# Spatial gating in three blocks: the norm's offset enters the base through column sums, and ScalarE normalises the second half's rows

## The chip, the cores and the metric

The kernel runs on one core of a Trainium2 chip. The metric is the device time of one execution in microseconds (us); a time quoted below is the median of three runs unless it is the profiled execution's own. The engines are TensorE (PE, with its weight loads as PEld), VectorE (DVE), ScalarE (ACT), GpSimd (POOL) and SyncE (SP), which here only issues DMAs.

## What is computed

The program applies three blocks of a network to 1024 positions of 1024 features. The change touches only the third, and in it the spatial gating:

```
def layer_norm(x, g, b):
    mu = jnp.mean(x32, axis=-1, keepdims=True)
    var = jnp.mean(jnp.square(x32 - mu), axis=-1, keepdims=True)
    y = (x32 - mu) * lax.rsqrt(var + EPS)
    return (y * g.astype(jnp.float32) + b.astype(jnp.float32)).astype(x.dtype)

def spatial_gating(u, v, ln_g, ln_b, w_s, b_s):
    """gMLP SGU: u * (W_s LN(v) + b) with W_s mixing positions inside each 128-chunk, per channel group."""
    v = layer_norm(v, ln_g, ln_b)
    vc = v.reshape(B, S // CHUNK, CHUNK, G_A, C // G_A)
    s = jnp.einsum('gpq,bcqge->bcpge', w_s, vc) + b_s.T[:, :, None]
    return u * s.reshape(B, S, C)
```

`v` is 1024 positions by 2048 channels, in 8 chunks of 128 positions and 16 groups of 128 channels. For an element, W_s LN(v) is the sum over positions q of w[p,q] (n[q] g + b), with n the normalised row. The part with `b` is b times the sum of w[p,q] over q, and does not depend on the chunk.

## The kernel before, in words

`spatial_gating` (line 3885) is called twice, for half 0 and half 1 of the channels (8 groups, 1024 channels each), with a dense layer between and one behind. Each call is a stage with a block of its own: every engine has its list of instructions, and the next stage starts when all have ended theirs. A tile t is one chunk of 128 positions; there are 8 tiles, and most buffers are doubled (`v_`, `raw`, `y`, the PSUM banks 2p and 2p+1), the gates `uz` tripled.

Per tile, the engines do this:

- **SyncE** (from line 3897) loads `raw` (the rows of v; all 2048 channels in half 0, since the variance needs them, 1024 in half 1) and `uz`, the factor u silu(z). `load_rows(t)` waits until norm(t-2) is through; `load_gates(t)` waits for gate(t-3). In its list come rows 0, the bias, `g`, `b`, the spatial weights `ws`, gates 0, rows 1, gates 1 and 2, and then for t from 2: rows t, gates t+1. Rows t+1 therefore stand behind gates t+1.
- **ScalarE** lays `base` into the two PSUM banks of the tile (`lay_base`, line 3941), in half 0 takes the sum of squares of `raw` and its root (`squares`, line 3948), and rounds the result to `high` (`rounds`, line 3956). In the loop the order is lay_base(t+1), squares(t+2), rounds(t).
- **VectorE** normalises (`norm`, line 3995) and multiplies the mixed result by `uz` (`gate`, line 4009), in the order norm(t+1), gate(t). `norm` is two three-input instructions of 128x1024: (raw + less) times g at line 3998, then times rstd plus b at line 4006. In half 0 the reciprocal of the root stands between them (line 4003). `less` is minus the mean; `rstd` is left over from half 0 for half 1.
- **TensorE** mixes: eight plain float32 matmuls of 128x128 per tile (line 4049), which add into the base.
- **POOL** subtracts `high` from the result to give `low` (line 3981, 128x1024); gate(t+2) waits for it.

At the start TensorE spreads the bias over 128 partitions by matmuls with one contracted row (line 4038), from the bias split in two parts, and ScalarE copies the result to `base` (line 3964).

```
                    v.wait_ge(sig(f"loaded{p}"), j * 16 + 16)
                    v.wait_ge(sig("mixed"), t * 2 + 2)
```

These two waits head `norm`: `mixed` is preset to 4, so that norm(0) and norm(1) do not wait for a matmul.

Of the kernel before, what the change touches and what calls it, by code (L numbers as in the profile page):

```python
# [8 lines left out]
P = 128  # L9
# [3 lines left out]
NT = SEQ // P  # L13
HALF = 512
# [6 lines left out]
ALU = mybir.AluOpType  # L21
ACT = mybir.ActivationFunctionType
# [655 lines left out]
class Stage:  # L678
# [15 lines left out]
    def sb(self, name, shape, dt=F32):  # L694
        return self.ctx.enter_context(self.core.nc.sbuf_tensor(f"{self.name}_{name}_sb", shape, dt))
# [3190 lines left out]
def spatial_gating(core, half, sums, less, rstd, high, low, weights):  # L3886

    nc, d = core.nc, core.d
    with Stage(core, f"sgu{half}") as st:
# [1 line left out]
        ws = sb("ws", [P, GH, P])  # L3891
        bias = [st.sb(f"bias{i}", [1, GH * P], F32R) for i in range(2)]
        one = st.sb("one", [1, P], F32R)
        g, b_ = (sb(n, [P, DH])[:, :] for n in ("g", "b"))
        v_ = [sb(f"v{p}", [P, DH]) for p in range(2)]
        raw = [sb(f"raw{p}", [P, DA if half == 0 else DH]) for p in range(2)]
        uz = [sb(f"uz{i}", [P, GH, P]) for i in range(3)]
# [2 lines left out]
        var = sb("var", [P, NT]) if half == 0 else None  # L3900
        mine = slice(half * DH, (half + 1) * DH)
        gs = slice(half * GH, (half + 1) * GH)
        base = sb("base", [P, GH * P])
        with nc.Block() as block:
            @block.sync
            def _(sp):
                def load_rows(t, p, j):
                    if t >= 2:
                        sp.wait_ge(sig("normed"), t - 1)
                    of = d["rows3"][ds(t * P, P), VA:VA + DA] if half == 0 else d["rows3"][ds(t * P, P), VA + DH:VA + DA]  # L3910
                    sp.dma_start(raw[p][:, :], of).then_inc(sig(f"loaded{p}"), 16)

                def load_gates(t):
                    if t >= 3:
                        sp.wait_ge(sig("done"), t)
                    sp.dma_start(uz[t % 3][:, :, :], d["uz"][mine, ds(t * P, P)].rearrange("(k p) t -> p k t", p=P)
                                 ).then_inc(sig(f"gates{t % 3}"), 16)
                load_rows(0, 0, 0)
                sp.dma_start(bs, d["b_spatial"][0:1, gs, :].rearrange("o g t -> o (g t)")).then_inc(sig("bias_in"), 16)
                for to, of in ((g, d["sgu_g"][:, mine]), (b_, d["sgu_b"][:, mine])):  # L3920
                    sp.dma_start(to, of).then_inc(sig("affine_in"), 16)
                sp.dma_start(ws[:, :, :], d["w_spatial"][:, gs, :]).then_inc(sig("spatial_in"), 16)
                load_gates(0)
                load_rows(1, 1, 0)
                load_gates(1)
                load_gates(2)
                for t in range(2, NT):
                    load_rows(t, t % 2, t // 2)
                    if t + 1 < NT:
                        load_gates(t + 1)  # L3930

            @block.scalar
            def _(a):
# [6 lines left out]
                def lay_base(t, p):  # L3940
# [4 lines left out]
                        ins = nc.scalar.activation(core.acc[2 * p + q][:, :], base[:, q * HALF:(q + 1) * HALF], ACT.Copy)  # L3945
                    ins.then_inc(sig("based"), 1)

                def squares(t, p, j):
                    a.wait_ge(sig(f"loaded{p}"), j * 16 + 16)
                    nc.scalar.activation(core.acc_quad, raw[p][:, :], ACT.Square, bias=less[:, ds(t, 1)],  # L3950
# [8 lines left out]

                if half == 0:  # L3960
                    squares(0, 0, 0)
                a.wait_ge(sig("spread"), 1)
                for q in range(2):
                    ins = nc.scalar.activation(base[:, q * HALF:(q + 1) * HALF], core.acc[q][:, :], ACT.Copy)
# [2 lines left out]
                lay_base(0, 0)  # L3967
                if half == 0:
                    squares(1, 1, 0)
                for t in range(NT):  # L3970
                    if t + 1 < NT:
                        lay_base(t + 1, (t + 1) % 2)
                    if half == 0 and t + 2 < NT:
                        squares(t + 2, t % 2, t // 2 + 1)
                    rounds(t, t % 2)

            @block.gpsimd
# [8 lines left out]
            def _(v):  # L3986
                v.sem_inc(sig("done"), 2)
                v.sem_inc(sig("split"), 2)
                if half == 0:
# [2 lines left out]
                    nc.vector.tensor_scalar(less[:, :], less[:, :], -1.0 / DA, None, ALU.mult).then_inc(sig("less"), 1)  # L3992
                    v.wait_ge(sig("less"), 2)

                def norm(t, p, j):
                    v.wait_ge(sig(f"loaded{p}"), j * 16 + 16)
                    v.wait_ge(sig("mixed"), t * 2 + 2)
                    nc.vector.scalar_tensor_tensor(out=v_[p][:, :], in0=raw[p][:, mine] if half == 0 else raw[p][:, :],
                                                   scalar=less[:, ds(t, 1)], in1=g, op0=ALU.add,
                                                   op1=ALU.mult).then_inc(sig("centred"), 1)  # L4000
                    if half == 0:
                        v.wait_ge(sig("rooted"), t + 1)
                        nc.vector.reciprocal(rstd[:, ds(t, 1)], rstd[:, ds(t, 1)]).then_inc(sig("inverted"), 1)
                        v.wait_ge(sig("inverted"), t + 1)
                    v.wait_ge(sig("centred"), t + 1)
                    nc.vector.scalar_tensor_tensor(out=v_[p][:, :], in0=v_[p][:, :], scalar=rstd[:, ds(t, 1)], in1=b_,
                                                   op0=ALU.mult, op1=ALU.add).then_inc(sig("normed"), 1)

                def gate(t, p):
                    v.wait_ge(sig("split"), t + 1)  # L4010
# [21 lines left out]
            @block.tensor  # L4032
            def _(pe):
                pe.sem_inc(sig("mixed"), 4)
                pe.wait_ge(sig("bias_low"), 1)
                for q in range(2):
                    for i in range(2):
                        mm = nc.tensor.matmul(core.acc[q], one[:, :], bias[i][:, q * HALF:(q + 1) * HALF], start=i == 0, stop=i == 1)
                mm.then_inc(sig("spread"), 1)
                pe.wait_ge(sig("spatial_in"), 16)  # L4040

                def body(t, p, j):
                    pe.wait_ge(sig("based"), t + 1)
# [314 lines left out]
```

## Time and profile before

| | us |
|---|---|
| median of 3 runs | 4650.26 (4645.92 to 4656.61) |
| profiled execution, its own time | 4649.78 |
| its span, first to last instruction | 4648.0 |
| TensorE busy | 4284.1 (92%) |
| VectorE busy | 1886.4 (41%) |
| ScalarE busy | 1343.2 (29%) |
| POOL busy | 1154.4 (25%) |
| stretch 4094 to 4157.7, TensorE / VectorE / ScalarE / POOL busy | 28.9 / 35.3 / 38.6 / 21.0 |
| stretch 4282.5 to 4342.3, the same | 30.4 / 43.5 / 19.1 / 19.8 |

The two stretches are the two calls of `spatial_gating`. Times are microseconds from the start of the span. A row of the order of time reads: start, duration, engine, line, operation, names written and read, shapes, count, and in brackets how long the engine had been idle before it and what ended that. Where a row stands for several instructions, the duration runs from the first start to the last end. A mean granted TensorE clock of 1.00 is 2.4 GHz, 0.50 is 1.2 GHz.

### The profile page before, as it was taken

How to read it: one execution, taken by the hardware profiler on the slowest of the kernel's cores; microseconds unless marked ns; L12 is line 12 of the kernel's file. 1: busy time of each engine (PE TensorE's matmuls, PEld its weight loads, DVE VectorE, ACT ScalarE, POOL GpSimd, SP SyncE). 2: the span in 40 equal slices, each digit the busy share in tenths (PEclk: the TensorE clock that was granted, in tenths of full speed). 3: DMA queues.
4: the chain of work that ended last, by engine and by line, in shares of the span. 5: the costliest groups of instructions: out<-in, count | busy, mean ns of one | idle time of the engine just before them, and what ended most of it. 6: DMA issues, size and time to landing. Idle time of an engine off the chain costs nothing. (4 is left out here: it accounts for less than half of the span.)

```text
span 4648.0 us, 53906 instructions
## 1 busy us (share of the span) xinstructions
PE 4284.1 (92%) x21558; PEld 3501.7 (75%) x21558; DVE 1886.4 (41%) x3289; ACT 1343.2 (29%) x2357; POOL 1154.4 (25%) x575
## 2 busy tenths in 40 slices
PE   8999999879995888699999999999999999967897
PEld 6888777656775887468888877888788888856776
DVE  3022666652595665435424424000133333346433
ACT  3121333432313443421001012112244444343112
POOL 2220100331152666222222212212111111122313
PEclk9999999879997999899999999999999999978899
DMA  3243111331523110311111112333333333266422
GB/s 123 102 157 102 34 27 26 118 97 50 208 87 99 42 31 17 110 46 46 55 46 46 55 37 89 113 138 104 90 84 104 104 107 95 67 218 191 154 82 91
DMA packets 276997, 417.23 MB, mean 90 GB/s; under 512 B 50439, under 2 KB 184120, under 8 KB 270862
## 3 DMA queue, kind: packets, MB, share of 16 engines
q1 hardware_dynamic: 221022, 313.20, 21.8%
q10 hardware_dynamic: 53104, 94.92, 5.5%
q0 software_dynamic: 2624, 5.68, 0.5%
q8 instruction: 172, 2.82, 0.3%
q14 instruction: 75, 0.61, 0.0%
HBM read 290.31 MB, written 123.40 MB: 89 GB/s over the span
## 5 line engine op out<-in xcount | busy, mean ns | idle before, releaser
L163 POOL TENSOR_TENSOR weights_wlow<-weights_raw,weights_whigh 128x1024 fp32r<-128x1024 f32 (+1 forms) x236 | 695.6, 2969 | 2450.3 <-ACT weights_whigh L154 2450.3
L154 ACT ACTIVATE weights_whigh<-weights_raw 128x1024 fp32r<-128x1024 f32 (+1 forms) x236 | 266.6, 1164 | 1170.8 <-PE acc L313 787.8
L313 PE MATMUL acc<-h_high_half,weights_whigh 128*128 128x512 f32 x1408 | 556.8, 395 | 20.9 <-POOL weights_wlow L163 17.1
L313 PE MATMUL acc<-h_low_half,weights_whigh 128*128 128x512 f32 x1408 | 553.7, 393 | 0.0
L313 PE MATMUL acc<-h_high_half,weights_wlow 128*128 128x512 f32 x1408 | 553.5, 393 | 0.0
L313 PEld LDWEIGHTS acc<-h_high_half,weights_whigh 128*128 128x128 f32 x1408 | 266.0, 189 | 89.2 <-POOL weights_wlow L163 18.4
L3575 PE MATMUL acc<-h_high_half,weights_whigh 128*128 128x512 f32 x768 | 331.3, 431 | 0.0
L313 PEld LDWEIGHTS acc<-h_high_half,weights_wlow 128*128 128x128 f32 x1408 | 265.9, 189 | 59.3 <-issue 1.0
L313 PEld LDWEIGHTS acc<-h_low_half,weights_whigh 128*128 128x128 f32 x1408 | 265.6, 189 | 59.3
L3575 PE MATMUL acc<-h_low_half,weights_whigh 128*128 128x512 f32 x768 | 302.2, 393 | 0.0
L3575 PE MATMUL acc<-h_high_half,weights_wlow 128*128 128x512 f32 x768 | 300.8, 392 | 0.0
L316 PE MATMUL acc<-weights_whigh,h_low_half 128*128 128x512 f32 x768 | 300.3, 391 | 0.0
L316 PE MATMUL acc<-weights_wlow,h_high_half 128*128 128x512 f32 x768 | 300.3, 391 | 0.0
L316 PE MATMUL acc<-weights_whigh,h_high_half 128*128 128x512 f32 x768 | 300.3, 391 | 0.0
L313 PE MATMUL acc<-y_high_half,weights_whigh 128*128 128x512 f32 x448 | 181.8, 406 | 28.2 <-DVE x_here L4138 17.7
L2023 DVE TENSOR_TENSOR x_here<-x_here,acc 128x512 f32<-128x512 f32 x80 | 55.0, 687 | 371.2 <-PE acc L313 371.2
L313 PE MATMUL acc<-hidden_high,weights_whigh 128*128 128x512 f32 x512 | 199.2, 389 | 0.0
L313 PE MATMUL acc<-hidden_high,weights_wlow 128*128 128x512 f32 x512 | 199.2, 389 | 0.0
L3483 DVE SCALAR_TENSOR_TENSOR gated_biased_sb<-gated_near_ends_sb,gated_slope_sb,acc 128x384 f32<-128x384 f32 x40 | 24.6, 614 | 412.3 <-DMA gated_end_sb<-rows 271.0
L313 PE MATMUL acc<-y_high_half,weights_wlow 128*128 128x512 f32 x448 | 178.8, 399 | 0.0
L313 PE MATMUL acc<-y_low_half,weights_whigh 128*128 128x512 f32 x448 | 178.6, 399 | 0.0
L3500 ACT ACTIVATE gated_probs_sb<-gated_biased_sb,gated_result_sb 128x192 f32<-128x192 f32 (+2 forms) x192 | 85.4, 446 | 290.4 <-DVE gated_result_sb L3490 290.1
(555 smaller groups left out, 8238.9 us busy)
## 6 DMA issues: line engine op xcount, KB each, us to landing
weights_raw<-w_cols SPq DMA_DIRECT2D x94, 512.0 KB, 4.8
weights_raw<-w_ff SPq DMA_DIRECT2D x64, 512.0 KB, 3.7
weights_raw<-w_rows SPq DMA_DIRECT2D x30, 1024.0 KB, 7.2
att<-gated_result_sb SPq DMA_DIRECT2D x96, 130.0 KB, 2.2
merge_o_sb<-att SPq DMA_DIRECT2D x24, 520.0 KB, 6.6
rows<-norm_square ACTq DMA_DIRECT2D x48, 256.0 KB, 2.1
weights_raw<-w_out SPq DMA_DIRECT2D x24, 512.0 KB, 3.8
cols<-first_out ACTq DMA_DIRECT2D x40, 256.0 KB, 2.0
```

What stands on the lines that cost most here:

```text
L154: self.core.nc.scalar.activation(high[p][:, half * (KC // 2):(half + 1) * (KC // 2), :], raw[half], ACT.Copy).then_inc(self.core.sem("roun ...
L163: self.core.nc.gpsimd.tensor_tensor(low[p][:, hs, :], raw[half], high[p][:, hs, :].bitcast(F32), ALU.subtract).then_inc(self.core.sem("wei ...
L313: mm = nc.tensor.matmul(core.acc[b][:, :], wt[p][:, k, c * P:(c + 1) * P], h[:, k, half * HALF:(half + 1) * HALF], start=first, stop=final)
L316: mm = nc.tensor.matmul(core.acc[b][:, 0:width], h[:, k, b * P:(b + 1) * P], wt[p][:, k, :], start=first, stop=final)
L2023: return core.nc.vector.tensor_tensor(to, to, acc, ALU.add)
L3483: nc.vector.scalar_tensor_tensor(out=biased, in0=mask, scalar=self.slope[p][:, st["dilation"]:st["dilation"] + 1], in1=acc, op0=ALU.mult, ...
L3500: nc.scalar.activation(self.probs[g % 2][:, u, 0:w], self.biased[g % 2][:, u, 0:w], ACT.Exp, bias=result[:, u, AE + 1:AE + 2], scale=AE ** ...
L3575: mm = nc.tensor.matmul(core.acc[b][:, :], wt[n % 2][:, k, c * P:(c + 1) * P], of[:, k, half * HALF:(half + 1) * HALF], start=(k == 0 and ...
```

## The change

`b` is loaded as one row instead of 128. TensorE first multiplies a column of ones with the spatial weights (two matmuls of 512 columns, one output row), which gives the column sums; ScalarE copies them to the buffer `columns`; TensorE adds `b` times these sums to the spread bias, group by group (eight matmuls with one contracted row), before ScalarE takes the base. `norm` then needs no offset: in half 0 it is the reciprocal, a tensor_scalar (plus less, times rstd) and a multiplication by `g`, all behind the root; in half 1 ScalarE computes raw times rstd plus `shift` (`shift` is less times rstd) in place in `raw`, in the new function `centre`, and VectorE multiplies by `g`. The wait for the matmul of two tiles before stays with VectorE.

```diff
--- before.py
+++ after.py
@@ -3891,7 +3891,7 @@
         ws = sb("ws", [P, GH, P])
         bias = [st.sb(f"bias{i}", [1, GH * P], F32R) for i in range(2)]
         one = st.sb("one", [1, P], F32R)
-        g, b_ = (sb(n, [P, DH])[:, :] for n in ("g", "b"))
+        g, b_ = sb("g", [P, DH])[:, :], sb("b", [1, DH])[:, :]
         v_ = [sb(f"v{p}", [P, DH]) for p in range(2)]
         raw = [sb(f"raw{p}", [P, DA if half == 0 else DH]) for p in range(2)]
         uz = [sb(f"uz{i}", [P, GH, P]) for i in range(3)]
@@ -3900,7 +3900,8 @@
         var = sb("var", [P, NT]) if half == 0 else None
         mine = slice(half * DH, (half + 1) * DH)
         gs = slice(half * GH, (half + 1) * GH)
-        base = sb("base", [P, GH * P])
+        base, columns = sb("base", [P, GH * P]), y[1][0:1, :]
+        shift = sb("shift", [P, NT]) if half else None
         with nc.Block() as block:
             @block.sync
             def _(sp):
@@ -3917,7 +3918,7 @@
                                  ).then_inc(sig(f"gates{t % 3}"), 16)
                 load_rows(0, 0, 0)
                 sp.dma_start(bs, d["b_spatial"][0:1, gs, :].rearrange("o g t -> o (g t)")).then_inc(sig("bias_in"), 16)
-                for to, of in ((g, d["sgu_g"][:, mine]), (b_, d["sgu_b"][:, mine])):
+                for to, of in ((g, d["sgu_g"][:, mine]), (b_, d["sgu_b"][0:1, mine])):
                     sp.dma_start(to, of).then_inc(sig("affine_in"), 16)
                 sp.dma_start(ws[:, :, :], d["w_spatial"][:, gs, :]).then_inc(sig("spatial_in"), 16)
                 load_gates(0)
@@ -3945,6 +3946,12 @@
                         ins = nc.scalar.activation(core.acc[2 * p + q][:, :], base[:, q * HALF:(q + 1) * HALF], ACT.Copy)
                     ins.then_inc(sig("based"), 1)
 
+                def centre(t, p, j):
+                    a.wait_ge(sig(f"loaded{p}"), j * 16 + 16)
+                    a.wait_ge(sig("less"), 1)
+                    nc.scalar.activation(raw[p][:, :], raw[p][:, :], ACT.Identity, scale=rstd[:, ds(t, 1)],
+                                         bias=shift[:, ds(t, 1)]).then_inc(sig("centred"), 1)
+
                 def squares(t, p, j):
                     a.wait_ge(sig(f"loaded{p}"), j * 16 + 16)
                     nc.scalar.activation(core.acc_quad, raw[p][:, :], ACT.Square, bias=less[:, ds(t, 1)],
@@ -3959,6 +3966,12 @@
 
                 if half == 0:
                     squares(0, 0, 0)
+                else:
+                    centre(0, 0, 0)
+                a.wait_ge(sig("column_sums"), 1)
+                for q in range(2):
+                    ins = nc.scalar.activation(columns[:, q * HALF:(q + 1) * HALF], core.acc[2 + q][0:1, :], ACT.Copy)
+                ins.then_inc(sig("columns"), 1)
                 a.wait_ge(sig("spread"), 1)
                 for q in range(2):
                     ins = nc.scalar.activation(base[:, q * HALF:(q + 1) * HALF], core.acc[q][:, :], ACT.Copy)
@@ -3967,11 +3980,15 @@
                 lay_base(0, 0)
                 if half == 0:
                     squares(1, 1, 0)
+                else:
+                    centre(1, 1, 0)
                 for t in range(NT):
                     if t + 1 < NT:
                         lay_base(t + 1, (t + 1) % 2)
                     if half == 0 and t + 2 < NT:
                         squares(t + 2, t % 2, t // 2 + 1)
+                    if half and t + 2 < NT:
+                        centre(t + 2, t % 2, t // 2 + 1)
                     rounds(t, t % 2)
 
             @block.gpsimd
@@ -3992,19 +4009,20 @@
                     nc.vector.tensor_scalar(less[:, :], less[:, :], -1.0 / DA, None, ALU.mult).then_inc(sig("less"), 1)
                     v.wait_ge(sig("less"), 2)
 
+                if half:
+                    nc.vector.tensor_tensor(shift[:, :], less[:, :], rstd[:, :], ALU.mult).then_inc(sig("less"), 1)
+
                 def norm(t, p, j):
-                    v.wait_ge(sig(f"loaded{p}"), j * 16 + 16)
                     v.wait_ge(sig("mixed"), t * 2 + 2)
-                    nc.vector.scalar_tensor_tensor(out=v_[p][:, :], in0=raw[p][:, mine] if half == 0 else raw[p][:, :],
-                                                   scalar=less[:, ds(t, 1)], in1=g, op0=ALU.add,
-                                                   op1=ALU.mult).then_inc(sig("centred"), 1)
                     if half == 0:
+                        v.wait_ge(sig(f"loaded{p}"), j * 16 + 16)
                         v.wait_ge(sig("rooted"), t + 1)
                         nc.vector.reciprocal(rstd[:, ds(t, 1)], rstd[:, ds(t, 1)]).then_inc(sig("inverted"), 1)
                         v.wait_ge(sig("inverted"), t + 1)
+                        nc.vector.tensor_scalar(v_[p][:, :], raw[p][:, mine], less[:, ds(t, 1)], rstd[:, ds(t, 1)], ALU.add,
+                                                ALU.mult).then_inc(sig("centred"), 1)
                     v.wait_ge(sig("centred"), t + 1)
-                    nc.vector.scalar_tensor_tensor(out=v_[p][:, :], in0=v_[p][:, :], scalar=rstd[:, ds(t, 1)], in1=b_,
-                                                   op0=ALU.mult, op1=ALU.add).then_inc(sig("normed"), 1)
+                    nc.vector.tensor_tensor(v_[p][:, :], v_[p][:, :] if half == 0 else raw[p][:, :], g, ALU.mult).then_inc(sig("normed"), 1)
 
                 def gate(t, p):
                     v.wait_ge(sig("split"), t + 1)
@@ -4032,12 +4050,22 @@
             @block.tensor
             def _(pe):
                 pe.sem_inc(sig("mixed"), 4)
+                pe.wait_ge(sig("spatial_in"), 16)
+                for q in range(2):
+                    mm = nc.tensor.matmul(core.acc[2 + q][0:1, :], core.ones[:, 0:1], ws[:, 4 * q:4 * q + 4, :].rearrange("p g t -> p (g t)"),
+                                          start=True, stop=True)
+                mm.then_inc(sig("column_sums"), 1)
                 pe.wait_ge(sig("bias_low"), 1)
                 for q in range(2):
                     for i in range(2):
-                        mm = nc.tensor.matmul(core.acc[q], one[:, :], bias[i][:, q * HALF:(q + 1) * HALF], start=i == 0, stop=i == 1)
+                        nc.tensor.matmul(core.acc[q], one[:, :], bias[i][:, q * HALF:(q + 1) * HALF], start=i == 0, stop=i == 1)
+                pe.wait_ge(sig("affine_in"), 32)
+                pe.wait_ge(sig("columns"), 1)
+                for gg in range(GH):
+                    cs = slice(gg * P, (gg + 1) * P)
+                    mm = nc.tensor.matmul(core.acc[gg // 4][:, gg % 4 * P:(gg % 4 + 1) * P], b_[0:1, cs], columns[:, cs],
+                                          start=False, stop=True, skip_group_check=True)
                 mm.then_inc(sig("spread"), 1)
-                pe.wait_ge(sig("spatial_in"), 16)
 
                 def body(t, p, j):
                     pe.wait_ge(sig("based"), t + 1)
```

Three places show how the instructions stand. On **TensorE** at the start of each of the two stages (`sgu_ws` are the spatial weights, `sgu_one` ones, `sgu_y` holds the column sums):

```order
-L4038 MATMUL acc<-sgu_bias_sb,sgu_one_sb 128x512 x4
-L4049 MATMUL acc<-sgu_ws_sb,sgu_v_sb 128x128 x64
-L3904 UNCONDITIONAL_BRANCH
+L4050 UNCONDITIONAL_BRANCH
+L4055 MATMUL acc<-sgu_ws_sb,ones_here 1x512 x2
+L4061 MATMUL acc<-sgu_bias_sb,sgu_one_sb 128x512 x4
+L4066 MATMUL acc<-sgu_y_sb,sgu_b_sb 128x128 x8
+L4077 MATMUL acc<-sgu_ws_sb,sgu_v_sb 128x128 x64
```

Two matmuls now stand ahead of the bias and eight behind it; the 64 mixing matmuls are as before.

On **VectorE** in half 0, norm(2), gate(1) and norm(3), before:

```order
L3998 SCALAR_TENSOR_TENSOR sgu_v_sb<-sgu_raw_sb,va_less,sgu_g_sb 128x1024
L4003 RECIPROCAL va_rstd<-va_rstd 128x1
L4006 SCALAR_TENSOR_TENSOR sgu_v_sb<-sgu_v_sb,va_rstd,sgu_b_sb 128x1024
L4015 TENSOR_TENSOR sgu_y_sb<-acc,sgu_uz_sb 128x512 x2
L3998 SCALAR_TENSOR_TENSOR sgu_v_sb<-sgu_raw_sb,va_less,sgu_g_sb 128x1024
```

and in the change:

```order
L4020 RECIPROCAL va_rstd<-va_rstd 128x1
L4022 TENSOR_SCALAR sgu_v_sb<-sgu_raw_sb,va_less,va_rstd 128x1024
L4025 TENSOR_TENSOR sgu_v_sb<-sgu_v_sb,sgu_g_sb 128x1024
L4033 TENSOR_TENSOR sgu_y_sb<-acc,sgu_uz_sb 128x512 x2
L4020 RECIPROCAL va_rstd<-va_rstd 128x1
```

The first long instruction has moved behind the reciprocal, and so behind the root on ScalarE.

On **ScalarE** in half 1, from the start of the stage, in the change:

```order
L3937 ACTIVATE sgu_bias_sb<-sgu_y_sb 1x1024
L3952 ACTIVATE sgu_raw_sb<-sgu_raw_sb,sgu_shift_sb,va_rstd 128x1024
L3973 ACTIVATE sgu_y_sb<-acc 1x512 x2
L3977 ACTIVATE sgu_base_sb<-acc 128x512 x2
L3946 ACTIVATE acc<-sgu_base_sb 128x512 x2
L3952 ACTIVATE sgu_raw_sb<-sgu_raw_sb,sgu_shift_sb,va_rstd 128x1024
L3946 ACTIVATE acc<-sgu_base_sb 128x512 x2
L3952 ACTIVATE sgu_raw_sb<-sgu_raw_sb,sgu_shift_sb,va_rstd 128x1024
L3965 ACTIVATE y_high_half<-sgu_y_sb 128x8x128
```

The instructions of line 3952 and the pair of line 3973 are new; before, the rounding of a tile (there line 3958) stood directly behind the laying of the next.

## Rows read from the trace of the kernel before

**Rows 1.** The page: its first line.

```profile
span 4648.0 us, 53906 instructions
```

**Rows 2.** Order of time, first half, POOL: start us, us, engine line op, names, shapes.

```profile
4124.67 2.72 POOL L3981 TENSOR_TENSOR y_low_half<-sgu_y_sb,y_high_half 128x1024 fp32r<-128x1024 f32 x1 [1.97 <-ACT y_high_half L3958]
...
4155.21 2.34 POOL L3981 TENSOR_TENSOR y_low_half<-sgu_y_sb,y_high_half 128x1024 fp32r<-128x1024 f32 x1 [1.45 <-ACT y_high_half L3958]
```

**Rows 3.** Order of time, second half, POOL.

```profile
4307.24 2.34 POOL L3981 TENSOR_TENSOR y_low_half<-sgu_y_sb,y_high_half 128x1024 fp32r<-128x1024 f32 x1 [3.45 <-ACT y_high_half L3958]
...
4339.72 2.34 POOL L3981 TENSOR_TENSOR y_low_half<-sgu_y_sb,y_high_half 128x1024 fp32r<-128x1024 f32 x1 [1.08 <-ACT y_high_half L3958]
```

**Rows 4.** Order of time, first matmul behind the second half, TensorE.

```profile
4342.56 0.77 PE L313 MATMUL acc<-y_high_half,weights_whigh 128*128 128x512 f32 x1 [4.73 <-PEq L3904]
```

**Rows 5.** Order of time, first half, VectorE: gate(0), tile 3, gates 2 and 6.

```profile
4113.43 1.28 DVE L4015 TENSOR_TENSOR sgu_y_sb<-acc,sgu_uz_sb 128x512 f32<-128x512 f32 x2
...
4123.89 1.28 DVE L4006 SCALAR_TENSOR_TENSOR sgu_v_sb<-sgu_v_sb,va_rstd,sgu_b_sb 128x1024 f32<-128x1024 f32 x1
4125.10 1.28 DVE L4015 TENSOR_TENSOR sgu_y_sb<-acc,sgu_uz_sb 128x512 f32<-128x512 f32 x2
...
4148.96 1.28 DVE L4015 TENSOR_TENSOR sgu_y_sb<-acc,sgu_uz_sb 128x512 f32<-128x512 f32 x2
```

**Rows 6.** Order of time, first half, ScalarE, around the root of tile 3.

```profile
4121.22 1.97 ACT L3950 ACTIVATE acc<-sgu_raw_sb,va_less 128x2048 f32<-128x2048 f32 x1 [0.29 <-DMA sgu_raw_sb<-rows]
...
4123.35 0.30 ACT L3953 ACTIVATE va_rstd<-sgu_var_sb,eps_here 128x1 f32<-128x1 f32 x1
4123.55 1.04 ACT L3958 ACTIVATE y_high_half<-sgu_y_sb 128x1024 fp32r<-128x1024 f32 x1
```

**Rows 7.** Order of time, second half, VectorE.

```profile
4298.04 1.28 DVE L4015 TENSOR_TENSOR sgu_y_sb<-acc,sgu_uz_sb 128x512 f32<-128x512 f32 x2
...
4307.29 3.37 DVE L4006 SCALAR_TENSOR_TENSOR sgu_v_sb<-sgu_v_sb,va_rstd,sgu_b_sb 128x1024 f32<-128x1024 f32 x1
...
4333.85 1.27 DVE L4015 TENSOR_TENSOR sgu_y_sb<-acc,sgu_uz_sb 128x512 f32<-128x512 f32 x2
```

**Rows 8.** Instructions on the tile sgu_ws: issue of its loads, and landing.

```profile
L3922 SPq DMA_DIRECT2D sgu_ws_sb<-w_spatial x2: 432/497/562, 4097.1 to 4284.4; - x2
...
DMA to landing us min/median/max: 8.0/8.0/8.1
```

**Rows 9.** Order of time, first norm instruction of each half, VectorE.

```profile
4103.89 1.28 DVE L3998 SCALAR_TENSOR_TENSOR sgu_v_sb<-sgu_raw_sb,va_less,sgu_g_sb 128x1024 f32<-128x1024 f32 x1 [1.41 <-DMA sgu_b_sb<-sgu_b]
...
4291.09 1.28 DVE L3998 SCALAR_TENSOR_TENSOR sgu_v_sb<-sgu_raw_sb,va_less,sgu_g_sb 128x1024 f32<-128x1024 f32 x1 [2.77 <-DMA sgu_b_sb<-sgu_b]
```

**Rows 10.** Order of time, float32 matmuls of 512 columns elsewhere, TensorE.

```profile
1947.82 6.69 PE L3180 MATMUL acc<-second_sums_sb,ones_here 128*128 128x512 f32 x8 [29.25 <-DVE second_sums_sb L3247]
```

**Rows 11.** Windows: start:end, us, busy PE, PEld, DVE, ACT, POOL, granted clock, DMA, GB/s.

```profile
4346.00:4347.00 1.00, 1.00 (x4) 0.76 (x4) 0.00 (x0) 0.00 (x0) 0.00 (x0) 0.69 0.88 295
...
1953.00:1954.00 1.00, 1.00 (x4) 0.42 (x2) 0.74 (x2) 0.19 (x1) 0.00 (x0) 0.56 1.00 401
```

**Rows 12.** Order of time, first half, ScalarE: the copy of the base.

```profile
4104.66 1.06 ACT L3964 ACTIVATE sgu_base_sb<-acc 128x512 f32<-128x512 f32 x2
```

**Rows 13.** Order of time, first half, TensorE.

```profile
4102.53 2.07 PE L4038 MATMUL acc<-sgu_bias_sb,sgu_one_sb 1*128 1x512 f32 x4 [10.10 <-DVE sgu_bias_sb L4020]
4106.98 3.76 PE L4049 MATMUL acc<-sgu_ws_sb,sgu_v_sb 128*128 128x128 f32 x16 [2.38 <-ACT acc L3945]
...
4125.65 2.05 PE L4049 MATMUL acc<-sgu_ws_sb,sgu_v_sb 128*128 128x128 f32 x16 [0.89 <-ACT acc L3945]
```

**Rows 14.** Instructions of lines 1456 and 3263, VectorE (ns min/median/max, first and last start).

```profile
L1456 DVE TENSOR_SCALAR norm_square<-short_in,short_taps x6: 752/754/4031, 265.2 to 376.5; 128x1024 f32<-128x1024 f32 x6
...
L3263 DVE TENSOR_TENSOR second_y_sb<-second_y_sb,second_rstd_sb x4: 1215/1216/1216, 1963.4 to 1969.1; 128x1024 f32<-128x1024 f32 x4
```

**Rows 15.** DMA issues in the second half: engine op xcount, KB, us to landing.

```profile
sgu_raw_sb<-rows SPq DMA_DIRECT2D x8, 512.0 KB, 4.8
```

## The prediction

> **What bounds the kernel now.** I read the page first, for the span [rows 1], then the order of time of each engine over the two stretches in which the function `spatial_gating` runs, 4094 to 4158 us (first half of the channels) and 4282 to 4342 us (second half). Both are stages of their own: the last instruction of each is the last subtraction on GpSimd (POOL), ending at 4157.55 in the first [rows 2] and at 4342.06 in the second [rows 3], and TensorE's first matmul of the next stage starts 0.5 us later [rows 4]. So a microsecond won or lost in either stage is one of the whole time, and nothing else in the program changes.
>
> The **first half** is a loop over loads. The row load of tile t+1 stands on SyncE behind the gate load of that tile, which waits for the gate of tile t-2. So gate(0) lets rows 3 be loaded, these feed norm(3), which VectorE runs ahead of gate(2); gate(2) releases rows 5, and so on. From the rows: gate(0) ends at 4114.71 [rows 5], the squares of tile 3 start at 4121.22, when the DMA landed [rows 6], 6.51 later. Squares and root take 2.43, to 4123.65 [rows 6]; the second norm instruction starts 0.24 behind the root (4123.89) and the gate 1.21 behind that; the gate is 1.28 [rows 5]. 6.51 + 2.43 + 0.24 + 1.21 + 1.28 = 11.67 per two tiles, as gate(0) to gate(2) in the trace.
>
> The **second half** is bound by VectorE and POOL together. The second norm instruction takes 3.37 us where it starts 0.05 behind POOL's subtraction [rows 3, 7], against 1.28 alone [rows 5]; POOL's ends at 4309.59, VectorE's at 4310.66. An instruction with two SBUF inputs thus waits until POOL has finished, while gates, which read PSUM, stay at 1.28. Six gates lie 4333.85 - 4298.04 = 35.81 us apart, some 5.97 per tile, of which 2.1 is this wait.
>
> **Part 1: the start of each stage.** Before, TensorE needed only the bias to build the base. Now it first needs `ws`, the spatial weights, then column sums, ScalarE's copy, eight outer products and only then the base. `ws` was issued fifth and took 8.0 us to land, about 4105.2 and 4292.4 [rows 8]. The load of `b` ahead of it shrinks from 512 KB to 4 KB, so I let `ws` land when `b` did: about 4103.8 and 4291.0 [rows 9]. Bounds: no gain at all, 1.4 later in each half; I take the nearer row, since the order of issue stays.
>
> From there: two plain float32 matmuls of 512 columns. Four such take 6.69 with the clock mostly at 0.50 [rows 10, 11], so two take 3.4 and some 0.4 until the last result. Copying the sums is a pair of ScalarE copies as in [rows 12], 1.1 with its start. The four bias matmuls, 2.07 before [rows 13], lie beside that copy (3.4 + 1.7 = 5.1, against 5.0 for the copy). Then eight 128x128 float32 matmuls: 3.76 at the lower clock, 2.05 at the full one [rows 13]. TensorE comes cold (1.2 GHz). In [rows 11] the clock rose about 4 us after unbroken work began (start 4342.56 in [rows 4]), and after 6.1 us in the other case (start 1947.82). So the eight cost between 2.05 and 3.75; with a rise in their first third I take 2.4. TensorE is done 7.5 after the landing (7.1 to 8.9). Then the base copy and the laying of tile 0, a pair of copies each [rows 12], with their starts 2.3. Base laid at 4103.8 + 9.8 = 4113.6 and 4291.0 + 9.8 = 4300.8.
>
> *First half.* Squares(1) stand on ScalarE behind that laying. 4113.6 + squares and root 2.43 + reciprocal 0.24 + scale 0.85 + multiplication 1.14 + gate 1.28 = 4119.5 for the end of gate(0), against 4114.71: **+4.8**. *Second half.* Norms 0 and 1 are ready or early, the mixing takes 3.76 cold, and the last half of the gate 0.7: 4300.8 + 0.1 + 3.75 + 0.7 = 4305.3, against 4298.04 + 1.28 = 4299.3: **+6.0**.
>
> **Part 2: the norm of the first half.** Removed: the subtraction with gain, which ran beside the squares and was hidden, and the second three-input instruction (1.28). Added behind the root: a tensor_scalar with two scalars and a multiplication of two tensors. The first is bounded by 0.75, what 128x1024 takes with one scalar, and by 1.28, a three-input instruction; the second scalar adds what it adds between the two-tensor and the three-input form, 1.216 against 1.28 [rows 5, 14], so 0.81, plus 0.04 to the next start. The multiplication is 1.22 [rows 14]. Alone this makes a loop 0.85 - 0.06 = 0.8 longer.
>
> But it moves the multiplication into POOL's way. After the root ScalarE rounds the previous tile, and POOL starts 1.02 after the root's end (4123.65 to 4124.67) [rows 2, 6]. Before, VectorE's instruction had started at +0.24, ahead of POOL. Now the scale ends and the multiplication starts at 0.24 + 0.85 = +1.09, which is 0.07 behind POOL; 0.05 was enough to make it wait in [rows 3, 7]. POOL runs 2.35 and VectorE ends 1.02 after it (4310.66 - 4309.59 = 1.07, less 0.06): 1.02 + 2.35 + 1.02 = +4.39, instead of +1.52. The loop grows by 2.87 to 14.54. Three loops lie between gate(0) and gate(6): 43.6 against 4148.96 - 4113.43 = 35.5 [rows 5], **+8.1**. The tail behind gate(6) stays.
>
> The Trainium skill, "VectorE: DVE Perf Modes", Rules for kernel authors, advises to minimise the number of instructions, as each is followed by a drain. By that alone half one gets eight instructions more and half two eight fewer, and this loop would grow by 0.8 only, which is the sum of the first rival. "GPSIMD Engine Reference", Key points, has VectorE share SBUF interfaces with POOL when it has two SBUF inputs or runs in a two-port mode; the two-input case is what the rows of the second half show, the other no row of these stages does.
>
> **Part 3: the norm of the second half.** ScalarE centres and scales in place (128x1024, as its rounding: 1.04 [rows 6]), VectorE multiplies once. ScalarE has room, two copies and a rounding being all that it did per tile. POOL again starts 1.0 behind the centring, but the multiplication starts 0.05 behind it and is through first; the wait of 2.1 goes and POOL waits 0.2 instead. What is late next is the load: 0.44 for SyncE, 4.8 to land [rows 15], centring 1.05, 0.05, multiplication 1.14, gate 1.28 = 8.76 per two tiles. Three loops 26.3 against 35.8: **-9.5**. The last mixing (3.76) is now less covered, **+0.5**. Shift (8x128 elements), less bytes, and memory: nothing, they lie in the idle start.
>
> **Sum:** 4.8 + 8.1 = +12.9 in the first half, 6.0 - 9.5 + 0.5 = -3.0 in the second, +9.9. The profiled execution took 4649.78, the median is 4650.26, 0.5 apart. I set the sum on the median: **4660 us**. About 0.2% (9.3 us) is what a measurement of this kernel can tell from no change, so the likeliest case lies almost on that line.
>
> **The rivals.**
> *A. The multiplication is ahead of POOL* (not slower). Place: the first half, 1.02 us behind each root. It decides at 70 ns: if the scale takes 0.74 or less, the multiplication takes the port first and POOL waits. For it: the margin is as small as that. Against: in half two a lead of 0.05 was enough for POOL. Loop 12.46, three 37.4, +1.9 in place of +8.1: total +3.7, 4654.
> *B. The clock goes up in the start and stays up.* The mixing is then 2.05: in the second half the first and the last are on the path, 3.4 less: +6.5, 4657. For it: long unbroken work in the start. Against: the later mixings of both halves lie between 2.05 and 3.8 [rows 13].
> *C. The start stays at the lower clock throughout*: 8.9 instead of 7.5, twice: +12.7, 4663. If `ws` gains nothing from the shorter queue either, 2.8 more, 4666.
> *D. The narrow matmuls are cheap*, a column sum costing like a bias matmul (0.5): each start 3.5 shorter, +2.9, 4653. Nothing in the rows speaks for it but the small outputs.
>
> **How the numbers follow.** The forecast has 0.55, A 0.2, B 0.08, C 0.07, D 0.05, and 0.05 remain for what I do not see, a gain included. The range reaches from just below D and A less a run's scatter (the three runs spread over 10.7 us) to C with the late weights and a little scatter: 4649 to 4668; the forecast's own is 4655 to 4665. Slower by over 0.2%: a little over half of the forecast, all of C, 0.39 or 0.40. Faster by over 0.2%: 0.06, from scatter and the unseen. Within 0.2%: 0.54.
>
> **What would show it.** In the new trace: (1) `ws` lands near 4103.8 and 4291.0, column sums take 3.4; (2) gate(0) ends at 4119.5 and, shifted by the first half, 6.0 later than before in the second; (3) the new multiplication of the first half takes 3.3 us from tile 3 on, gates 14.5 apart in pairs; if it takes 1.22 and POOL 2.7, A holds; (4) in the second half multiplications take 1.22 and gates come in pairs 8.8 apart. The prediction is wrong if the first half is less than 8 us longer or the second is longer than before.

## The result, and the profile after

The change takes 4662.57 us, median of 13 runs (4656.91 to 4670.89), the kernel before 4648.17 in 13 runs beside it. The ratio is 1.0028, interval 1.0020 to 1.0035, which is 9 to 16 us with 13.0 in the middle (the two medians lie 14.4 apart): slower, and the interval begins just at the 0.2% that the prediction takes as its line. Forecast were +9.9 and 4660.

The page of the profiled execution (its own time 4659.25): its first lines, busy time and share of the span.

```profile
span 4657.3 us, 53999 instructions
...
PE 4285.3 (92%) x21598; PEld 3499.3 (75%) x21598; DVE 1864.4 (40%) x3282; ACT 1352.4 (29%) x2369; POOL 1155.6 (25%) x575
...
DVE  3022666652595664434424424000133333346333
ACT  3121333432214443420010022122244444443212
POOL 2220100341153666112222222212111111122313
```

Less work for VectorE (1864 against 1886 us), little more for the others, and a span 9.3 us longer: the loss is waiting. The table splits it by hand from the orders of time below and from [rows 2, 3, 5, 7], each time counted from the first DMA issue of its stage (before 4095.26 and 4282.84, after 4090.76 and 4294.09).

| us | first half: before, after, forecast of the difference | second half: before, after, forecast |
|---|---|---|
| to the end of gate(0) | 19.5, 23.5 (+4.0), +4.8 | 16.5, 24.0 (+7.5), +6.0 |
| from there to the end of gate(6) | 35.5, 45.0 (+9.5), +8.1 | 35.8, 27.0 (-8.8), -9.5 |
| from there to POOL's last end | 7.3, 6.6 (-0.7), 0 | 6.9, 6.7 (-0.3), +0.5 |
| stage | 62.3, 75.1 (+12.8), +12.9 | 59.2, 57.7 (-1.6), -3.0 |

The two stages are 11.2 us longer together. Outside them this execution was 2 us shorter than the one before, in stretches that the change does not touch. A stage alone varies by one or two microseconds between executions of the same code: the second one of the change lasted 57.7 us here and 58.2 to 59.8 in four runs below that leave it as it is. The -1.6 of the second half lies within that, the +12.8 of the first does not.

**The start.** TensorE in order of time, first half, then second:

```profile
4099.16 3.57 PE L4055 MATMUL acc<-sgu_ws_sb,ones_here 128*1 128x512 f32 x4 [11.23 <-DMA sgu_ws_sb<-w_spatial]
4102.66 1.41 PE L4061 MATMUL acc<-sgu_bias_sb,sgu_one_sb 1*128 1x512 f32 x4
4103.98 2.02 PE L4066 MATMUL acc<-sgu_y_sb,sgu_b_sb 1*128 1x128 f32 x16
4108.32 3.78 PE L4077 MATMUL acc<-sgu_ws_sb,sgu_v_sb 128*128 128x128 f32 x16 [2.33 <-ACT acc L3946]
...
4302.23 3.57 PE L4055 MATMUL acc<-sgu_ws_sb,ones_here 128*1 128x512 f32 x4 [9.16 <-DMA sgu_ws_sb<-w_spatial]
4305.73 2.07 PE L4061 MATMUL acc<-sgu_bias_sb,sgu_one_sb 1*128 1x512 f32 x4
4307.61 3.61 PE L4066 MATMUL acc<-sgu_y_sb,sgu_b_sb 1*128 1x128 f32 x16
```

and the clock over them (start:end, us, busy PE, granted clock, DMA share, GB/s):

```profile
4103.00:4104.00 1.00, 1.00 (x5) 0.92 1.15 315
4104.00:4106.00 2.00, 2.00 (x17) 1.00 1.21 309
...
4302.00:4305.00 3.00, 2.77 (x4) 0.50 1.07 355
4305.00:4308.00 3.00, 3.00 (x7) 0.50 1.17 308
4308.00:4311.20 3.20, 3.20 (x16) 0.50 0.30 114
```

The column sums start at 4099.16 and 4302.23, 8.4 and 8.1 us into the stage, when `ws` has landed (before, it landed 9.9 and 9.6 into the stage). The two of them cost 3.5 us together, at the lower clock throughout; four took 6.69 in [rows 10], where the clock rose towards the end. In the first half the mean of 0.92 from 4103 to 4104 puts the rise to 2.4 GHz at about 4103.15, 4.0 us after TensorE began, and the eight outer products took 2.02; TensorE was through after 6.8. In the second half the instructions are the same, but the clock stayed at 0.50 for the nine microseconds up to 4311.2 of unbroken work; the same eight took 3.61 and the block 9.0. The forecast had one value, 7.5, for both. The difference is no chance of one execution: in the five first halves with column sums the eight took 1.99 to 2.02, in the five second halves 3.61 or 3.62.

**The loop of the first half.** VectorE from gate(0) to gate(3), and gate(6); ScalarE around tile 3; POOL:

```profile
4112.93 1.28 DVE L4033 TENSOR_TENSOR sgu_y_sb<-acc,sgu_uz_sb 128x512 f32<-128x512 f32 x2
...
4123.57 0.16 DVE L4020 RECIPROCAL va_rstd<-va_rstd 128x1 f32<-128x1 f32 x1 [5.92 <-ACT va_rstd L3960]
4123.77 0.81 DVE L4022 TENSOR_SCALAR sgu_v_sb<-sgu_raw_sb,va_less,va_rstd 128x1024 f32<-128x1024 f32 x1
4124.61 3.27 DVE L4025 TENSOR_TENSOR sgu_v_sb<-sgu_v_sb,sgu_g_sb 128x1024 f32<-128x1024 f32 x1
4127.81 1.27 DVE L4033 TENSOR_TENSOR sgu_y_sb<-acc,sgu_uz_sb 128x512 f32<-128x512 f32 x2
...
4129.19 0.81 DVE L4022 TENSOR_SCALAR sgu_v_sb<-sgu_raw_sb,va_less,va_rstd 128x1024 f32<-128x1024 f32 x1
4130.04 1.23 DVE L4025 TENSOR_TENSOR sgu_v_sb<-sgu_v_sb,sgu_g_sb 128x1024 f32<-128x1024 f32 x1
...
4157.95 1.27 DVE L4033 TENSOR_TENSOR sgu_y_sb<-acc,sgu_uz_sb 128x512 f32<-128x512 f32 x2
```

```profile
4107.15 1.12 ACT L3946 ACTIVATE acc<-sgu_base_sb 128x512 f32<-128x512 f32 x2
...
4121.02 1.97 ACT L3957 ACTIVATE acc<-sgu_raw_sb,va_less 128x2048 f32<-128x2048 f32 x1 [4.70 <-DMA sgu_raw_sb<-rows]
...
4123.14 0.29 ACT L3960 ACTIVATE va_rstd<-sgu_var_sb,eps_here 128x1 f32<-128x1 f32 x1
4123.35 1.04 ACT L3965 ACTIVATE y_high_half<-sgu_y_sb 128x1024 fp32r<-128x1024 f32 x1
...
4136.37 1.97 ACT L3957 ACTIVATE acc<-sgu_raw_sb,va_less 128x2048 f32<-128x2048 f32 x1 [5.19 <-DMA sgu_raw_sb<-rows]
```

```profile
4124.46 2.34 POOL L3998 TENSOR_TENSOR y_low_half<-sgu_y_sb,y_high_half 128x1024 fp32r<-128x1024 f32 x1 [5.85 <-ACT y_high_half L3965]
4130.25 3.23 POOL L3998 TENSOR_TENSOR y_low_half<-sgu_y_sb,y_high_half 128x1024 fp32r<-128x1024 f32 x1 [3.45 <-ACT y_high_half L3965]
...
4163.52 2.34 POOL L3998 TENSOR_TENSOR y_low_half<-sgu_y_sb,y_high_half 128x1024 fp32r<-128x1024 f32 x1 [0.78 <-ACT y_high_half L3965]
```

The root of tile 3 ends at 4123.43; the reciprocal starts 0.14 behind it. The scale takes 0.81 and ends at 4124.58, the multiplication starts at 4124.61, 0.15 behind POOL (4124.46), and takes 3.27 instead of 1.23. In tile 4 (4130.04) it starts 0.21 ahead of POOL and takes 1.23, and POOL 3.23 instead of 2.34. Compare [rows 5, 2], where the instruction in this place had started 0.78 ahead of POOL.

**The loop of the second half.** VectorE at gate(0), tile 3 and gate(6); ScalarE and POOL at the same place:

```profile
4317.36 0.69 DVE L4033 TENSOR_TENSOR sgu_y_sb<-acc,sgu_uz_sb 128x512 f32<-128x512 f32 x1 [0.77 <-PE acc L4077]
...
4324.75 1.22 DVE L4025 TENSOR_TENSOR sgu_v_sb<-sgu_raw_sb,sgu_g_sb 128x1024 f32<-128x1024 f32 x1 [4.36 <-ACT sgu_raw_sb L3952]
4325.89 1.28 DVE L4033 TENSOR_TENSOR sgu_y_sb<-acc,sgu_uz_sb 128x512 f32<-128x512 f32 x2
...
4343.79 1.28 DVE L4033 TENSOR_TENSOR sgu_y_sb<-acc,sgu_uz_sb 128x512 f32<-128x512 f32 x2
```

```profile
4323.40 1.24 ACT L3952 ACTIVATE sgu_raw_sb<-sgu_raw_sb,sgu_shift_sb,va_rstd 128x1024 f32<-128x1024 f32 x1 [3.25 <-DMA sgu_raw_sb<-rows]
4324.55 1.04 ACT L3965 ACTIVATE y_high_half<-sgu_y_sb 128x1024 fp32r<-128x1024 f32 x1
```

```profile
4325.67 2.52 POOL L3998 TENSOR_TENSOR y_low_half<-sgu_y_sb,y_high_half 128x1024 fp32r<-128x1024 f32 x1 [4.09 <-ACT y_high_half L3965]
...
4349.41 2.34 POOL L3998 TENSOR_TENSOR y_low_half<-sgu_y_sb,y_high_half 128x1024 fp32r<-128x1024 f32 x1 [0.81 <-ACT y_high_half L3965]
```

The multiplication (4324.75, 1.22) has a lead of 0.92 on POOL, and POOL waits 0.2 in its place (2.52 instead of 2.34). The 3.37 of [rows 7] is gone. Centring takes 1.24, not the 1.04 of a rounding, and what it waited for was the load of the rows.

### The profile page after: what moved, and what is told of

The parts are those of the page before. It is cut to its first block and busy times, and to the rows that moved or that the text cites. A ratio compares the mean times of both kernels' runs of the same rounds, so it can differ in the third digit from the quotient of the medians.

```text
span 4657.3 us, 53999 instructions
## 1 busy us (share of the span) xinstructions
PE 4285.3 (92%) x21598; PEld 3499.3 (75%) x21598; DVE 1864.4 (40%) x3282; ACT 1352.4 (29%) x2369; POOL 1155.6 (25%) x575
```

## The experiments

All were timed in five rounds beside the kernel before, and the ratios are to that kernel; a difference in us is the ratio times its time. "Stage" is again from the first DMA issue to POOL's last end, in one profiled execution each.

**One half at a time.** With `new` choosing between the old and the new code of `norm`, of the start and of `centre` (in part; in the second of the two runs `new` is `half in (1,)`):

```diff
+        new = half in (0,)
...
+                    if not new:
+                        return norm_old(t, p, j)
```

> Only the first half of the channels is changed, the second is the kernel before. My theory (a longer start, and VectorE's multiplication held up by POOL's subtraction behind each root): the first stage lasts 75 us from its first DMA issue to POOL's last subtraction, as with the whole change, against 62.3 before, the second 59.2 as before; time 12.8 us above the kernel before. Rival (the halves disturb each other, or the loss lies elsewhere in the program): the time is as with the whole change or the two halves alone don't add up to it.

Measured: 1.0023 (1.0014 to 1.0032), +10.7 us; stages 75.6 and 58.6.

> Only the second half of the channels is changed. My theory: its longer start (+7.5 us to the first gate) is a little more than paid back by the wait for POOL that goes (-9): stage 57.7 us against 59.2, the time 1.5 us below the kernel before, which can't be told from no change. Rival (the start is all that counts, the loop being bound by loads before as well): 5 us or more above.

Measured: 0.9999 (0.9990 to 1.0009); second stage 58.2. (The first one, not changed, was 64.4 in this execution, 2 us longer than in the two others that have it unchanged.) So the whole loss belongs to the first half, and the second is worth nothing that can be told, its start eating what its loop gives: its stage lasted 57.7, 58.2, 59.1, 59.1 and 59.8 in the five executions with the code of the change, and 59.2 and 58.6 in two with the code before.

**POOL a little later.** One useless ScalarE copy ahead of each rounding of the first half (in part):

```diff
                 def rounds(t, p):
                     a.wait_ge(sig("done"), t + 3)
+                    if half == 0:
+                        nc.scalar.activation(idle[:, ds(t * 48, 48)], core.ones[:, 0:48], ACT.Copy)
```

> The whole change plus one small, useless ScalarE copy of 128x48 ahead of each rounding in the first half, some 0.25 us, so that POOL's subtraction starts that much later. My theory (the multiplication starts 0.15 us behind POOL and waits for it): the multiplication now starts first and takes 1.23 instead of 3.27 us, POOL waits, three loops get some 2 us shorter each, the first stage falls from 75 to about 69.5 us and the time to 6 us below the whole change, although work was added. Rival (the loop is longer because of the number and length of the instructions behind the root): the multiplication stays at 3.27, or the stage gets no shorter, and longer by up to 1 us.

Measured: 1.0021 (1.0012 to 1.0029), stage 76.1. By the letter this went to the rival. But the copy had moved POOL by only 0.13 us. The multiplication of tile 3:

```profile
4121.18 3.40 DVE L4028 TENSOR_TENSOR sgu_v_sb<-sgu_v_sb,sgu_g_sb 128x1024 f32<-128x1024 f32 x1
```

and POOL:

```profile
4121.16 2.35 POOL L4001 TENSOR_TENSOR y_low_half<-sgu_y_sb,y_high_half 128x1024 fp32r<-128x1024 f32 x1 [5.90 <-ACT y_high_half L3968]
```

POOL was still ahead, by 0.02 us, and VectorE waited for it to the end. The run had not separated the two theories, only brought the margin down to the edge. The next has three copies of 16 columns each.

> As the run with one small ScalarE copy ahead of the rounding in the first half, but with three copies of 128x16. One copy moved POOL's start only 0.13 us, to 0.02 ahead of the multiplication, which still waited (3.40 us). Three should move it some 0.4, to 0.25 us behind the multiplication's start. My theory (whichever of the two starts first holds the other up until it has ended): the multiplication takes 1.23 us and POOL's subtraction 3.2, the first stage falls from 75 to about 70 us, the time to 5 us below the whole change. Rival (POOL goes first whatever the order of start, or the length of the chain behind the root is what counts): the multiplication stays above 3 us, the stage at 75 or more.

Measured: 1.0017 (1.0008 to 1.0026), +7.9 us; first stage 69.4. VectorE and POOL at tile 3:

```profile
4124.63 0.81 DVE L4026 TENSOR_SCALAR sgu_v_sb<-sgu_raw_sb,va_less,va_rstd 128x1024 f32<-128x1024 f32 x1
4125.48 1.23 DVE L4029 TENSOR_TENSOR sgu_v_sb<-sgu_v_sb,sgu_g_sb 128x1024 f32<-128x1024 f32 x1
```

```profile
4125.64 3.28 POOL L4002 TENSOR_TENSOR y_low_half<-sgu_y_sb,y_high_half 128x1024 fp32r<-128x1024 f32 x1 [6.05 <-ACT y_high_half L3969]
```

Now the multiplication is 0.16 ahead; it takes 1.23, in all eight tiles, and POOL 3.28. With 0.4 us of work added per tile the stage is 5.7 us shorter than with the change (75.1), 6.7 shorter than with one copy. The place in the order of start, not the length of the chain, costs these microseconds. The intervals of the whole times of this run and the change overlap, so the stage carries the verdict; the three executions in which POOL goes first had 75.1, 75.6 and 76.1, so that the 5.7 stands clear of what a stage varies by. From gate(0) to gate(6) it is 38.9 us, between the 35.5 before and the 45.0 of the change: some 3.3 us of the loss are left with the order put right, and no run here splits them between the longer chain behind the root and the loads.

**Only the scaling behind the root** (in part; the first of the two stands ahead of the wait for the root).

```diff
+                        nc.vector.scalar_tensor_tensor(out=v_[p][:, :], in0=raw[p][:, mine], scalar=less[:, ds(t, 1)], in1=g,
+                                                       op0=ALU.add, op1=ALU.mult).then_inc(sig("centred"), 1)
...
+                        nc.vector.tensor_scalar(v_[p][:, :], v_[p][:, :], rstd[:, ds(t, 1)], None, ALU.mult).then_inc(sig("normed"), 1)
```

> The whole change, but in the first half VectorE computes (raw + less) g in one instruction beside the squares, as before the change, and behind the root only the multiplication by rstd (tensor_scalar with one scalar). My theory: that one takes 0.75 us, starts 0.24 behind the root and is through before POOL starts at 1.0; the loop is 11.67 - 0.53 = 11.1 us per two tiles, three loops 33.5 (before 35.5, with the change 45.0), the first stage 62.3 + 4.0 - 2.0 = 64.3 us, the whole time 1 us above the kernel before. Rival (column sums and what they delay are the main loss): the stage stays above 70 us.

Measured: 0.9999 (0.9990 to 1.0008); stages 62.2 and 59.8. VectorE at gate(0), the scaling of tile 3 and gate(6), and POOL's start in tile 3:

```profile
4113.10 1.33 DVE L4036 TENSOR_TENSOR sgu_y_sb<-acc,sgu_uz_sb 128x512 f32<-128x512 f32 x2
...
4123.77 0.76 DVE L4025 TENSOR_SCALAR sgu_v_sb<-sgu_v_sb,va_rstd 128x1024 f32<-128x1024 f32 x1
...
4146.81 1.28 DVE L4036 TENSOR_TENSOR sgu_y_sb<-acc,sgu_uz_sb 128x512 f32<-128x512 f32 x2
```

```profile
4124.56 2.37 POOL L3998 TENSOR_TENSOR y_low_half<-sgu_y_sb,y_high_half 128x1024 fp32r<-128x1024 f32 x1 [5.63 <-ACT y_high_half L3965]
```

The scaling takes 0.76 here (0.75 in the other tiles) and is through at 4124.53, 0.03 us before POOL comes; whether an instruction with one tensor from SBUF would have had to wait, this run does not show. From gate(0) to gate(6) it is 33.7 us, as expected (33.5); gate(0) ends 22.0 into the stage instead of 23.5, because the chain behind the root is shorter there too, which the expectation had left out. This removes the whole loss without touching the column sums.

**The offset without column sums.** One matmul per group, `b` on all partitions times the spatial weights, gives b times the sum directly (in part; `b` is loaded on 128 partitions again, and the bias matmuls wait for nothing else):

```diff
-                    mm = nc.tensor.matmul(core.acc[gg // 4][:, gg % 4 * P:(gg % 4 + 1) * P], b_[0:1, cs], columns[:, cs],
+                    mm = nc.tensor.matmul(core.acc[gg // 4][:, gg % 4 * P:(gg % 4 + 1) * P], b_[:, cs], ws[:, gg, :],
```

> The whole change, but the offset enters the base by one matmul per group straight from b on all 128 partitions (128x128 by 128x128, out[c,p] = sum over q of b[c] w[q,p]), without column sums, ScalarE's copy of them and outer products; the bias matmuls need not wait for the spatial weights; b is loaded as 512 KB again. My theory of the start (each step behind the landing of the weights delays the first gate): base laid 16.0 us behind the stage's start instead of 17.5 in the first half, 15.7 instead of 19.4 in the second, time 5 us below the whole change. Rival (the start is hidden by loads and the loops): no change against it.

Measured: 1.0009 (1.0000 to 1.0018), +4.2 us; stages 73.5 and 53.6 instead of 75.1 and 57.7. TensorE in the second half:

```profile
4298.21 2.07 PE L4052 MATMUL acc<-sgu_bias_sb,sgu_one_sb 1*128 1x512 f32 x4 [6.55 <-DVE sgu_bias_sb L4034]
4301.85 3.69 PE L4057 MATMUL acc<-sgu_ws_sb,sgu_b_sb 128*128 128x128 f32 x16 [1.57 <-DMA sgu_ws_sb<-w_spatial]
4307.86 5.46 PE L4068 MATMUL acc<-sgu_ws_sb,sgu_v_sb 128*128 128x128 f32 x32 [2.32 <-ACT acc L3946]
```

The first mixing starts 15.2 us into the stage (first issue at 4292.67), 4.3 earlier than with the change (19.5), and the stage is 4.1 shorter, and shorter than any of the five with column sums: in the second half the start is paid in full. In the first half only 1.6 comes back, no more than a stage varies by; there six multiplications instead of three took 3.27, the earlier start having moved the even tiles behind POOL as well.

> First half as in the kernel before; second half as in the change with the direct offset matmuls, and the spatial weights and b loaded ahead of g. My theory: first stage 62.3 us, second about 54 (57.7 with the change, 59.2 before), time 5 us below the kernel before. Rival (no gain, since the loads of the next tiles set the loop): within 2 us of it.

Measured: 0.9982 (0.9973 to 0.9991), -8.4 us; stages 62.3 and 51.7. The second stage is 7.5 us shorter than before, which is nearly the whole gain.

> Both halves: direct offset matmuls; the order of loads at the start is bias, spatial weights, b, rows 0, g; in the first half (raw + less) g beside the squares and only the scaling by rstd behind the root. My theory: first stage 59 to 60 us (62.3 before), second 53 to 54 (59.2), time 8 us below the kernel before, about 0.17%. Rival (rows 0 now land later and hold the first tile up): stages as with scaling last and column sums, 62 and 58, no gain.

The direct matmuls in both halves and the scaling last in the first, with the bias, the weights and `b` loaded before rows 0 and `g`. Measured: 0.9982 (0.9973 to 0.9991), -8.4 us, 4641.4. The first issue of a stage is now that of the bias, not that of rows 0. SyncE at the start of both stages, and the last rows of POOL in both:

```profile
4095.85 0.26 SPq L3919 DMA_DIRECT2D sgu_y_sb<-b_spatial  x1
...
4285.38 0.25 SPq L3919 DMA_DIRECT2D sgu_y_sb<-b_spatial  x1
```

```profile
4154.89 2.34 POOL L3994 TENSOR_TENSOR y_low_half<-sgu_y_sb,y_high_half 128x1024 fp32r<-128x1024 f32 x1 [1.58 <-ACT y_high_half L3965]
...
4335.66 2.34 POOL L3994 TENSOR_TENSOR y_low_half<-sgu_y_sb,y_high_half 128x1024 fp32r<-128x1024 f32 x1 [1.37 <-ACT y_high_half L3965]
```

The stages are 61.4 and 52.6 us. ScalarE in the first half shows what the new order of loads does:

```profile
4104.41 1.97 ACT L3957 ACTIVATE acc<-sgu_raw_sb,va_less 128x2048 f32<-128x2048 f32 x1 [6.06 <-DMA sgu_raw_sb<-rows]
...
4108.02 1.06 ACT L3973 ACTIVATE sgu_base_sb<-acc 128x512 f32<-128x512 f32 x2
```

Rows 0 now land 8.6 us into the stage (before, the squares began 5.8 into it), and the copy of the base stands behind their squares and root: TensorE was done with it at 4105.20, the copy began at 4108.02. So the mechanism of the rival is there in the first half, and the stage misses its 59 to 60, though the gain as a whole came out at the 8 us expected.

Both of the last two versions have intervals that lie below the kernel before and well below the change, by 0.18% and by 0.46%. Between them nothing can be told: their stages add up to 114.0 us in both, against 121.5 before. The last run changed the loads, the start and the norm of the first half at once, and its first stage is only 0.9 us shorter than before, less than a stage varies by.

## Why the prediction was right

**What bounds.** Right as far as it was tried: the loss and the gain lie in the two stages, and the whole time follows them (+11.2 in the stages and +13.0 with the change, -7.5 and -8.4 with the second half direct).

**Part 1, the start.** Right in sign and kind, +4.0 and +7.5 for +4.8 and +6.0. The weights landed where `b` had [rows 9], within 0.2 us. The term that was mis-sized is the eight outer products: 2.4 was put for both halves between ends of 2.05 and 3.75, and the trace had 2.02 in one and 3.61 in the other. TensorE was through after 6.8 and 9.0 us where 7.5 stood for both, so one half came out 0.8 too long and the other 1.5 too short; that these nearly cancel in the sum is luck. Why the clock rose after 4.0 us in one half and not within 9 in the other, with the same instructions, no run here settles. The direct matmuls show the price of the start by its removal: 4.1 us in the second half.

**Part 2, the norm of the first half.** Right, and the term that decided. The scale took 0.811 where 0.81 was put together from one scalar more, and POOL's lead was 0.15 where 0.07 had been worked out, since the reciprocal came 0.14 behind the root instead of 0.06. A lead of 0.07 worked out from terms of that size could have fallen either way, and the prediction said so by its rival A. From the end of the root to the end of the gate tile 3 took 5.65 us instead of 2.73, 2.92 more for a forecast of 2.87; the three loops took 45.0 against 43.6. Of the 1.4 beyond it 1.3 is the loads: from gates 0, 2 and 4 to the next squares it took 6.8, 7.3 and 6.7 instead of 6.5. Rival A fell with it; moving POOL 0.3 us (the run with three copies) is A made true on purpose, and brought 5.7 of the 6.2 us by which forecast and rival differed.

The prediction also weighs a rule of "VectorE: DVE Perf Modes" in the Trainium skill (Rules for kernel authors), to keep the number of instructions low, and says that by it the first half gets eight instructions more. That count is wrong: a norm of the first half has three instructions before and after, and only the part behind the root has one more. The run with three copies leaves VectorE's instructions as they are and takes 5.7 us off the stage, so that their number is not the cause of those. "GPSIMD Engine Reference" of the Trainium skill, Key points, names the contention of two SBUF inputs with GpSimd; the 3.27 against 1.23 agree. That the one that starts second waits for the other's end is from these rows.

**Part 3, the norm of the second half.** Right in the loop, -8.8 for -9.5: the wait for POOL went and the load came next, with 1.24 instead of 1.05 for centring. The tail had +0.5 and was -0.3. A longer second half was to be a sign that the prediction is wrong; the profile after has it 1.6 shorter, but over the executions above no gain can be told.

**Rivals B, C, D.** Neither B nor C as a whole: in the start the first half had B's rise of the clock, the second C's lower one throughout. D fell: the column sums cost 1.75 each. Its 3.5 per start does not follow from its own price either, since two at 0.5 in place of 3.4 are 2.4 less.

**The sum.** +9.9 forecast, +11.2 in the stages of the profile, +13.0 by the ratio of the whole times, with 9 to 16 as interval; what is between the last two is within what one execution varies by. The prediction gave 0.54 to a result within 0.2% and 0.39 or 0.40 to a slower one. It came out slower, but the likeliest value had been put almost on the line, so that the argument hardly decides between the two.

## What to carry to other kernels

When a VectorE instruction with two tensors from SBUF and a GpSimd one from SBUF come up at about the same time, look at which of the two starts first: here 0.02 us decided over 2 us of waiting in every second tile. Before an instruction is moved behind another engine's result, write down what starts when behind the same event; an edit that makes the chain shorter is worth more than its own time if it moves it ahead of the other engine. A constant that is folded into the start of a stage is paid once in full where no load covers it: compute it by the fewest dependent steps. Its inputs should land early, but not ahead of the rows that the first tile needs, as the last run shows.

## What was not expected of the hardware

- The hand-over has no tolerance that these runs could find: a lead of 0.02 us of POOL cost VectorE 2.17 us (3.40 instead of 1.23), a lag of 0.16 cost it nothing and POOL 0.94 (3.28 instead of 2.34). Between these two no start was measured.
- The granted clock stayed at 0.50 through 9.0 us of unbroken TensorE work in the second half and rose after 4.0 us of the same work in the first. Rows of the kernel before had 4.1 and 6.1.
- ScalarE's activation with a bias and a scale from memory took 1.24 us on 128x1024, against 1.04 for the copy that rounds.
